# The value product of differential decode attention, computed in four column strips of TensorE

## What is computed

```python
# one decode token attends to K = 1024 + 1 cached rows; 2 KV heads n, 2 query heads g, 2 maps m, head width 64
s = einsum('bqngmd,bknmd->bngmqk', qb, kd) * 64 ** -0.5 - slope * dist
p = masked_softmax(s)
a = p[:, :, :, 0] - lam * p[:, :, :, 1]
o = einsum('bngqk,bknv->bqngv', a, vd)        # vd: (K, 2 heads, 128 value columns)
```

## Time and profile before

| | |
|---|---|
| median of three runs | 2085.61 us (2082.68 to 2092.02) |
| the profiled execution, from first to last instruction (no other time is recorded for it) | 2086.2 us |
| TensorE busy (MATMUL records) | 1972.7 us, 95% |
| VectorE, ScalarE, GpSimd busy | 1163.0, 678.2 and 152.2 us |
| granted TensorE clock, mean | 0.970 of full |
| TensorE busy between 180 and 500 us | 316.99 of 320 us |

### The profile page before, as it was taken

How to read it: one execution, slowest core, us unless ns; L and a number is a source line. 1 busy time by engine, 2 the same in 40 slices (tenths; PEclk the granted TensorE clock), 3 DMA queues, 4 the chain that set the end, 5 groups by cost and what they waited for, 6 DMA issues and landing times. The chain is left out here.

```text
span 2086.2 us, 34791 instructions
## 1 busy us (share of the span) xinstructions
PE 1972.7 (95%) x13032; PEld 1856.5 (89%) x13032; DVE 1163.0 (56%) x2531; ACT 678.2 (33%) x1273; POOL 152.2 (7%) x190
## 2 busy tenths in 40 slices
PE   5889999999997799999998999999999999999997
PEld 4658798789996688898898999999999999999997
DVE  4944333334244677777775546655556565555555
ACT  5623243331223566666573133311111110101011
POOL 1442100101300100000200000000000000000000
PEclk8799999999998899999899999999999999999999
DMA  9776453521001000000003541221212020211102
GB/s 311 255 215 205 152 180 98 156 94 60 30 26 66 1 1 1 1 1 1 1 1 102 173 131 50 62 61 30 60 30 60 30 60 30 60 31 59 40 0 82
DMA packets 151758, 157.10 MB, mean 75 GB/s; under 512 B 15859, under 2 KB 132483, under 8 KB 151604
## 3 DMA queue, kind: packets, MB, share of 16 engines
q1 hardware_dynamic: 140076, 130.73, 20.4%
q0 software_dynamic: 4656, 16.40, 2.3%
q10 hardware_dynamic: 6912, 8.46, 1.1%
HBM read 139.33 MB, written 18.32 MB: 76 GB/s over the span
## 5 line engine op out<-in xcount | busy, mean ns | idle before, releaser
L1877 DVE SCALAR_TENSOR_TENSOR l_x2T<-tail_bank,g_modT,l_x2T 128x344 f32<-128x344 f32 (+1 forms) x528 | 265.3, 566 | 101.5 <-PE tail_bank L1614 101.3
L1614 PE MATMUL tail_bank<-l_wo 128*128 128x344 f32 x1584 | 270.2, 319 | 1.8 <-DVE late_total_s L1883 1.8
L1614 PEld LDWEIGHTS tail_bank<-l_wo 128*128 128x128 f32 x1584 | 252.7, 188 | 2.0 <-issue 2.0
L1448 ACT ACTIVATE l_act<-tail_bank 128x344 f32<-128x344 f32 x66 | 30.2, 457 | 523.6 <-PE tail_bank L1596 523.6
L884 PE MATMUL nsa_out<-zs_z,nsa_probT 128*128 128x64 f32 (+1 forms) x1344 | 176.1, 277 | 5.3 <-DVE zs_z L1040 5.1
L884 PEld LDWEIGHTS nsa_out<-zs_z,nsa_probT 128*128 128x128 f32 x1344 | 169.1, 198 | 7.1 <-DVE zs_z L1040 7.0
L1596 PE MATMUL tail_bank<-late_words_hi,l_uhi 128*128 128x344 f32 x528 | 169.7, 321 | 3.3 <-DVE late_words_lo L1780 3.3
L1596 PE MATMUL tail_bank<-late_words_lo,l_uhi 128*128 128x344 f32 x528 | 169.3, 321 | 0.0
L1596 PE MATMUL tail_bank<-late_words_hi,l_ulo 128*128 128x344 f32 x528 | 169.2, 320 | 0.0
L1596 PE MATMUL tail_bank<-late_words_lo,late_wo 128*128 128x344 f32 x528 | 169.1, 320 | 0.0
L1596 PE MATMUL tail_bank<-late_words_hi,l_wo 128*128 128x344 f32 x528 | 169.1, 320 | 0.0
(11 more groups left out here) (504 smaller groups left out, 4329.2 us busy)
## 6 DMA issues: line engine op xcount, KB each, us to landing
mod_wr<-in_w_ada SPq DMA_DIRECT2D x24, 1024.0 KB, 5.3
kin_kin<-in_cache_kv SPq DMA_DIRECT2D x64, 256.0 KB, 3.4
late_gate<-in_w_ffn_in SPq DMA_DIRECT2D x22, 512.0 KB, 5.7
l_raw_o<-in_w_ffn_out SPq DMA_DIRECT2D x22, 512.0 KB, 3.6
late_raw<-in_w_ffn_in SPq DMA_DIRECT2D x22, 512.0 KB, 5.4
gate_d<-dec_gate ACTq DMA_DIRECT2D x48, 172.0 KB, 2.9
late_gate<-gate_d SPq DMA_DIRECT2D x8, 1032.0 KB, 5.5
dec_vin<-in_cache_kv SPq DMA_DIRECT2D x64, 128.0 KB, 2.2
```

The costliest lines, as they stand in the source:

```text
L1448: act.activation(sg[(j + c) % 2], pg[(j + c) % 2][:, 0:TCH], ACT.Silu).then_inc(silu_done, 1)
L1614: mm = pe.matmul(po[u % 4][:, 0:TCH], w[j][:, k * P:(k + 1) * P], a[j][:, tok(c)], start=(q == 0), stop=(q == 2))
L1877: mm = dve.scalar_tensor_tensor(out=here, in0=po[u % 4][:, 0:part_w(c)], scalar=g.modT[:, 5 * KD + k, NDEC:NC9], in1=here, op0=ALU.mult, o ...
```

## The change

The 512 columns of each product are no longer written by one matmul to partitions 0 to 15, but by four matmuls of 128 columns, each to a partition range of its own: 0, 32, 64 and 96 and the 15 after it, all in columns 0 to 127 of the bank. The stationary operand is the same for the four. The order is t outside, strip inside. DVE reads block i at partition 32 i instead of at column 128 i.

```diff
-  pe.matmul(odf[0:R, :], sco[:, S_DIF + t * R:S_DIF + (t + 1) * R], vin[:, :, t, :], start=(t == 0), stop=False)
+  for i in range(4):
+      pe.matmul(odf[32 * i:32 * i + R, 0:P], sco[:, S_DIF + t * R:S_DIF + (t + 1) * R],
+                vin[:, i // 2, t, i % 2 * P:i % 2 * P + P], start=(t == 0), stop=False)
   if part == 3:
-      pe.matmul(odf[0:R, :], new(S_DIF + NPAGE * R), vnew[:, 256:768], start=False, stop=True).then_inc(pv, 1)
+      for i in range(4):
+          mm = pe.matmul(odf[32 * i:32 * i + R, 0:P], new(S_DIF + NPAGE * R), vnew[:, 256 + i * P:256 + (i + 1) * P],
+                         start=False, stop=True)
+      mm.then_inc(pv, 1)
...
-  o, a = o16[:, 3 * HD:5 * HD], odf[0:R, i * P:(i + 1) * P]
+  o, a = o16[:, 3 * HD:5 * HD], odf[32 * i:32 * i + R, 0:P]
```

## The result

The changed kernel took 2073.78 us (median of 12 runs, 2060.18 to 2080.14) against 2088.9 us for the kernel before in the same comparison (12 runs, 2082.59 to 2093.26). The ratio is 0.9926, with a 95% interval of 0.9909 to 0.9942: faster by 15 us. Forecast were 2072 us and 13.9 us. The number is right by luck, since its working is not: the errors nearly cancel. The changed steps gave 22.8 us, not 13.9, and about 6 us of that went to a lower TensorE clock, which I had not in the sum. The kernel before came out 3.3 us above the 2085.61 that I had started from.

The account below looks back on a forecast made before the run. TensorE was taken to bound the kernel; half overlap saves 3.48 us a pair, 13.9 us over four, other costs 0: 2086.2 - 13.9 = 2072.3, less 0.6 to the median, said as 2072 us; range 2060 to 2090.

Parts of the forecast that it names:

- What bounds the kernel: Decode, 180 to 500 us: TensorE busy 316.99 of 320 us, so each microsecond saved there comes off the end.
- The old steps' cost: Parts 2 and 3 of a pair before the change: 3.54 and 4.50 us, 8.04 us a pair, 32.2 us in all.
- the rate of one record after the other: Records of 128 moving columns, one after the other on one strip: starts 0.110 us apart.
- if matmuls start in program order, the chain is then one slot for each source matmul and not two: Parts 2 and 3: second record holds up next strips; 1.96 and 2.60 us, saving 3.48 us a pair.
- the second rival: All four strips stream at once in parts 2 and 3: 0.97 and 1.28 us, 23.2 us saved, 2062.4 us; chance 0.18.
- My lower bound of a slot: Least cost of sending a record in the new steps: 0.027 us between starts, taken from line 2356.
- the half overlap: Parts 2 and 3: second record overlaps the next strip's first, halving the time; 13.9 us saved, chance 0.42.
- The costs put at nothing: Around the changed steps: 216 more weight loads, VectorE's reads at other partitions, DMA slack and gate feeding, 0 us taken.
- cover: End of the decode block, last pair: VectorE idles 4.93 us for TensorE, so a loss up to 4.9 us is covered.
- The third rival: Each of 36 strip changes a pair costs 0.09 to 0.10 us without overlap: 14.3 us more, 2100 us; chance 0.16.
- the 0.09 us: Price of a change of shape between matmuls, where the weight load comes late behind an idle gap.

Follow-up runs that it names:

- c2: Changed kernel with strip outside and t inside, so four or five source matmuls follow each other on one strip: 2078.32 us, ratio 0.9954.
- c3: Changed kernel plus 16 and 20 dense filler matmuls behind parts 2 and 3 in all pairs, results unread: 2088.75 us, ratio 1.0006.
- d3: Changed kernel plus the dense filler matmuls in the second pair alone: 2072.12 us, ratio 0.9915.
- d4: Changed kernel plus the dense filler matmuls in the last pair alone: 2073.26 us, ratio 0.9919.
- d1: Changed kernel with two strips of 256 columns in place of four of 128: 2078.32 us, ratio 0.9944.
- c4: Changed kernel with the products with the cached values left out, so its result is not the model's: 2059.45 us, ratio 0.9866.
- d2: Changed kernel plus two strips each for the compressed keys, the selected values and the window values: 2058.85 us, ratio 0.9855.
- e2: Changed kernel plus 29 sparse f32 matmuls of four moving columns in the last pair: 2078.45 us, ratio 0.9956.
- e1: Changed kernel with two t of one strip following each other, four records in a row on a strip: 2073.59 us, ratio 0.992.

## Why the prediction was right, and where it was wrong

What bounds the kernel: right. Every microsecond taken from these steps came off the end at equal clock, 22.4 for 22.8, and the same holds in all rows of the table above to about 2 us.

The old steps' cost, 8.04 us a pair, was right, and so was the rate of one record after the other, 0.110 us: c2's records inside a strip start 0.109 apart.

The step that failed is "if matmuls start in program order, the chain is then one slot for each source matmul and not two". In the changed kernel they did not start so across strips: four records started within 20 ns (241.204 to .224) and the next four 0.119 us after the first ones. As I read these starts, the second record of a source matmul waited for its strip, and TensorE meanwhile started records of other strips that stand behind it. Part 2 took 1.00 us where this step gave 1.96; the second rival, all four at once, had 0.97, and 23.2 us in all against 22.8 measured. I had given it 0.18, because I took the two records of a matmul to hold up the next strips. My lower bound of a slot rested on taking the 0.027 us of line 2356 for the least distance of two starts. That is not the least: records on different strips started 7 ns apart, and the 26 ns of the mean are a quarter of a slot.

That strips overlap at all stood in no row of the kernel before. It was my assumption, and so was the half overlap in the sum: no run shows its one slot of 0.110 us for each source matmul. What the trace of the changed kernel shows in its place is the four source matmuls of a t in two slots of 0.109 us, with 7 ns between the starts inside a bunch. The start in program order was assumed too; c2's interleaved starts, sorted as above, do not fit it.

The second missing term is the clock. The text said nothing of it beyond the 0.99 of the decode. It cost about 6 us. Had I put the strips right and left the clock out, the forecast would have been 2062.4 and 11 us too low: 6 for the clock, 3.3 for a kernel before that is slower than my three runs of it said, and 2 that I leave to the scatter of medians. The range would still have held it. So it is luck that 13.9 came near 15.1: 9 us too little for the steps against 6 us of clock left out, and the scatter.

The costs put at nothing were right: the 216 more weight loads went along inside the 1.00 us, VectorE's reads grew by 6 ns, the loads behind `pv` made no wait, and no cover was used up. The third rival, a change of shape at each change of strip, is out: the 0.09 us is paid on entering and leaving the group (240.96 to 241.20) and nowhere inside.

Open stays why the clock is lower. Shown is that it is (0.9663 against 0.9699), that it costs what is missing, that the strips as such don't do it (c3), and that with 6.0 us of dense filler in the second or in the fourth pair it is 0.9695 and 0.9690 (d3, d4). How much dense time went does not put the clocks in order: 12 us less than before gave 0.9693 (c2), 15.4 gave 0.9677 (d1), 22.8 gave 0.9663, 31 gave 0.9680 (c4) and 36 gave 0.9668 (d2). Whether the filler works because dense work was added or because what follows was shifted is not settled by e2.

## What to carry to other kernels

Look for products with few stationary columns, here 16 where the gate matmuls beside them have 128. The moving columns, split over four output partition ranges, went through 3.5 times as fast (3.54 to 1.00 us with all that is around it), and with 64 stationary columns in two strips nearly twice as fast (3.67 to 1.97 us), at the price of an offset in the reader. Put the strips next to each other in program order, or at most four records of one strip in a row: part 2 took 1.00 us with two in a row, 1.03 with four (e1) and 2.34 with eight (c2), which lost about half of the gain (10.8 of 22.4 us at equal clock). Between four and eight nothing was measured.

When a gain on the bounding engine doesn't arrive, put time against mean granted clock, run by run, before looking for a wait: here two lines 22.4 us apart lay under medians 12 to 19 us apart.

## What was not expected of the hardware

An f32 matmul's two records did not block other strips here: with four strips all eight records of a t went in two bunches, 0.109 us apart and 7 ns between starts. Part 2 kept its time with four records of a strip in a row (1.03 us, e1) and not with eight (2.34 us, c2).

The runs of one kernel differed mostly by the clock: 0.001 of mean granted clock is worth 1.5 to 1.8 us of some 2080, and about the line the scatter is 1.4 to 1.7 us.

6.0 us of added useless matmuls did not change the median (2072 to 2073 against 2068 to 2075 without them).
